# Modulation blocks summed on VectorE ahead of one ones-product, in a decoder trunk with 32 experts

## What is computed

```
mod = SiLU(c) @ w_ada + b_ada          # 6144 columns: shift, scale, gate of two sub-layers
h   = rms(x) * (1 + scale_mix) + shift_mix
z   = h @ w_in                          # [sc_x | sc_B | sc_C | u | v | gate_A | gate_B], 7 x 1024 columns
m   = sigmoid(gate_A) * sc_B * conv3(sc_C * sc_x) + sigmoid(gate_B) * gelu(u) * spatial(LN(gelu(v)))
x   = x + gate_mix * (m @ w_out)
h   = rms(x) * (1 + scale_ffn) + shift_ffn
x   = x + gate_ffn * MoE(h)             # top 4 of 32 experts; then a final norm
```

## Time and profile before

| | |
|---|---|
| median of 3 runs | 1212.75 us (1208.46 to 1213.37) |
| the profiled execution's own time | 1212.76 us |
| its span, first to last instruction | 1211.0 us |
| mean granted TensorE clock | 0.954 |
| TensorE, VectorE, ScalarE busy | 968.6, 452.8, 400.4 us |
| moved by DMA | 467.52 MB, mean 386 GB/s |

### The profile page before, as it was taken

How to read it: one execution, slowest core, us unless ns; L and a number is a source line. 1 busy time by engine, 2 the same in 40 slices (tenths; PEclk the granted TensorE clock), 3 DMA queues, 4 the chain that set the end, 5 groups by cost and what they waited for, 6 DMA issues and landing times.

```text
span 1211.0 us, 23871 instructions
## 1 busy us (share of the span) xinstructions
PE 968.6 (80%) x9321; PEld 495.8 (41%) x9322; DVE 452.8 (37%) x1137; ACT 400.4 (33%) x773; POOL 9.7 (1%) x29
## 2 busy tenths in 40 slices
PE   5999999998688788789689778577587576686586
PEld 3788989853233233234224323123132132132132
DVE  0655654664244244233324324223233233242243
ACT  1544424524243233323324324223223223232234
POOL 0200000000000000000000000000000000000000
PEclk9999999999999899999979989999899899899899
DMA  9979488799989999999997999999999999999993
GB/s 361 376 282 345 171 319 297 293 370 427 425 363 421 426 397 398 425 424 376 425 428 309 426 427 426 426 425 426 428 426 426 426 428 424 425 426 426 425 425 141
DMA packets 60356, 467.52 MB, mean 386 GB/s; under 512 B 5148, under 2 KB 6468, under 8 KB 24484
## 3 DMA queue, kind: packets, MB, share of 16 engines
q1 hardware_dynamic: 60324, 467.06, 93.7%
HBM read 466.00 MB, written 1.05 MB: 386 GB/s over the span
## 4 chain that ended last, share of the span: by engine, by line
PE 48%; DMA 35%; SPq 8%; issue 4%; DVE 4%; ACT 1%; ACTq 0%
DMA W<-in_w_down_dram 33%; PE B L1272 24%; PE B L1019 15%; SPq L385 6%; PE B L1281 3%; PE B L1039 2%; DMA raw<-in_w_in_dram 1%; SPq L387 1%; PE B L1224 1%; DMA raw<-in_w_ada_dram 1%; DVE EW L955 1%; DVE EW L952 1%; DVE EW L958 1%; ACT EW L634 1%; PE B L1287 0%
## 5 line engine op out<-in xcount | busy, mean ns | idle before, releaser
L1272 PE MATMUL B<-W,mT 128*32 128x256 f32 (+1 forms) x5888 | 544.5, 515 | 150.4 <-DMA W<-in_w_gate_up_dram 109.4
L1272 PEld LDWEIGHTS B<-W,mT 128*32 128x32 f32 x5888 | 197.9, 112 | 472.0 <-issue 192.4
L644 ACT ACTIVATE hT<-hT 32x256 bf16<-32x256 bf16 x368 | 152.6, 415 | 241.4 <-DVE hT L972 233.6
L952 DVE TENSOR_SCALAR EW<-B 128x256 f32<-128x256 f32 x46 | 19.5, 425 | 405.3 <-PE B L1272 405.3
L634 ACT ACTIVATE EW<-EW 128x256 f32<-128x256 f32 x46 | 19.2, 416 | 353.7 <-DVE EW L952 353.7
L1019 PE MATMUL B<-hh,wh 128*128 128x256 f32 x384 | 109.9, 286 | 0.0
L1019 PE MATMUL B<-hl,wh 128*128 128x256 f32 x384 | 108.6, 283 | 0.0
L1019 PE MATMUL B<-hh,wl 128*128 128x256 f32 x384 | 108.6, 283 | 0.0
L717 DVE TENSOR_TENSOR wl<-raw,wh 128x2048 fp32r<-128x2048 f32 x32 | 72.7, 2312 | 72.7 <-ACT wh L528 72.7
L1281 PE MATMUL B<-b_gu,mT 128*32 128x512 f32 x368 | 50.2, 614 | 59.9 <-issue 48.4
L528 ACT ACTIVATE wh<-raw 128x2048 fp32r<-128x2048 f32 x32 | 59.6, 1907 | 110.7 <-DMA raw<-in_w_in_dram 76.3
(11 more groups left out here) (241 smaller groups left out, 728.0 us busy)
## 6 DMA issues: line engine op xcount, KB each, us to landing
W<-in_w_gate_up_dram SPq DMA_DIRECT2D x128, 2048.0 KB, 33.6
W<-in_w_down_dram SPq DMA_DIRECT2D x63, 2048.0 KB, 24.8
raw<-in_w_in_dram SPq DMA_DIRECT2D x13, 2048.0 KB, 8.4
raw<-in_w_ada_dram SPq DMA_DIRECT2D x11, 2048.0 KB, 12.1
raw<-in_w_out_dram SPq DMA_DIRECT2D x2, 2048.0 KB, 10.8
W<-in_w_ada_dram SPq DMA_DIRECT2D x1, 2048.0 KB, 24.1
raw<-in_w_in_dram SPq DMA_DIRECT2D x2, 1024.0 KB, 17.0
W<-in_w_down_dram SPq DMA_DIRECT2D x2, 1024.0 KB, 20.4
```

Source lines behind the costliest of these rows:

```text
L644: A(ys[CAP * m:CAP * m + CAP, g * QC:(g + 1) * QC], yp[CAP * g:CAP * g + CAP, m, :], ACT.Copy).then_inc(y_moved, 1)
L952: V.tensor_scalar(halves(gs), paired(GU[:, 0:QC]), LIMIT, None, ALU.min).then_inc(gmin_ready, 1)
L1272: t = M(o, src[:, k % KQ, CAP * (k // KQ):CAP * (k // KQ) + CAP], w, start=(first and k == 0), stop=(k == KT - 1))
```

## The change

The eight units of blocks 1 and 2 are no longer multiplied on TensorE. VectorE weighs them: `weigh(i, q)` multiplies the 128 rows of a contraction step by their 128 values of SiLU(c) (`cT`, one scalar a partition) and adds them into a new tile `weighed` of 128 x 2048. One unit is two instructions; the first of a block writes (TENSOR_SCALAR), all others add (SCALAR_TENSOR_TENSOR). After four units what is left is the sum over 128 partitions, and `sum_weighed(i)` makes it with four matmuls against a tile of ones (`cond[:, 0, :]`, set to 1.0 after block 0 is done). The weighing of a unit stands in VectorE's stream one section ahead of the place that the unit had on TensorE: unit (1, 0) between the splits for SC_C and SC_X; units 1 to 3 of a half behind block 0 of sections 0 to 2; unit (2, 0) behind block 0 of GATE_B of the first half. `ada_used`, which frees the ring slot, now comes from VectorE for these units. Room for `weighed` is made by a smaller scratch for DMA descriptors. The order of the transfers is as before.

```diff
@@ VectorE
+            def weigh(i, q):
+                n = unit_no[("ada", i, q)]
+                dve.wait_ge(*landed(n))
+                if q == 0 and i > 1:
+                    dve.wait_ge(ada_summed, i - 1)
+                w = raw_slot(n).rearrange("p (k j n) -> p k j n", k=2, j=4)
+                if q == 0:
+                    step(V.tensor_scalar(weighed[:, :, :], w[:, 0], cT[:, 0:1], None, ALU.mult))
+                else:
+                    step(V.scalar_tensor_tensor(weighed[:, :, :], w[:, 0], cT[:, 2 * q:2 * q + 1], weighed[:, :, :], ALU.mult, ALU.add))
+                V.scalar_tensor_tensor(weighed[:, :, :], w[:, 1], cT[:, 2 * q + 1:2 * q + 2], weighed[:, :, :], ALU.mult, ALU.add).then_inc(ada_used, 1)
+                dve.wait_ge(ada_used, 4 * i + q + 1)
+                if q == 3:
+                    dve.nop().then_inc(weighed_ready, 1)
...
-                dve.wait_ge(ada_used, 4 * (i + 1))
+                if i == 0:
+                    dve.wait_ge(ada_used, 4)
+                else:
+                    dve.wait_ge(ada_summed, i)
...
             add_bias(0)
+            V.memset(cond[:, 0, :], 1.0).then_inc(ones_ready, 1)
...
-            for j in range(1, 4):
+            for j in range(1, 3):
                 split_low(j)
+            weigh(1, 0)
+            split_low(3)
...
+                        if b == 0 and n < 3:
+                            weigh(1 + h, n + 1)
+                        if b == 0 and s == GATE_B and h + 1 < NH:
+                            weigh(2 + h, 0)
@@ TensorE
+            def sum_weighed(i):
+                if i == 1:
+                    pe.wait_ge(v_gelu, TA * NH)
+                    pe.wait_ge(ones_ready, 1)
+                if i == 2:
+                    pe.wait_ge(mod_ready, 2)
+                pe.wait_ge(weighed_ready, i)
+                for j in range(4):
+                    t = M(B[7][32 * j:32 * j + 32, :], cond[:, 0, :], weighed[:, j, :], start=True, stop=True)
+                t.then_inc(ada_summed, 1)
...
-                        if b == 0 and i < 4:
-                            modulation(1 + h, i)
                     if s == U_:
                         spatial(2 * h + 1)
+                        sum_weighed(1 + h)
@@ build
-    nc = _bacc.Bacc("TRN2", target_bir_lowering=False, num_devices=1)
+    nc = _bacc.Bacc("TRN2", target_bir_lowering=False, num_devices=1, dynamic_dma_scratch_size=2048)
```

More of the change, by code:

```diff
@@ L111, in hybrid_trunk @@
         stat = sb("stat", [P, 64])
+        weighed = sb("weighed", [P, 4, HALF])
         def slot(n, k=1):
@@ L233, in hybrid_trunk @@
         s_slot = [sem(f"s_slot{n}") for n in range(RING)]
-        ada_used = sem("ada_used"); split_h = sem("split_h"); split_l = sem("split_l")
+        ada_used = sem("ada_used"); weighed_ready = sem("weighed_ready"); ada_summed = sem("ada_summed"); ones_ready = sem("ones_ready"); split_h = sem("split_h"); split_l = sem("split_l")
         c_ident = sem("c_ident"); c_iota = sem("c_iota"); c_pcol = sem("c_pcol"); c_late = sem("c_late"); pool_step = sem("pool_step")
@@ L1029, in modulation @@
                     pe.wait_ge(cond_ready, 1)
[L1030 to L1033, removed]
                 n = unit_no[("ada", i, q)]
```

## The result

| | before | after |
|---|---|---|
| median, first comparison | 1210.83 us (4 runs) | 1198.74 us (4 runs) |
| ratio, 95% interval | | 0.990 [0.9873, 0.9927] |
| median, second comparison | 1209.69 us (23 runs) | 1199.06 us (6 runs) |
| ratio, 95% interval | | 0.9906 [0.9886, 0.9926] |
| profiled execution, its own time | 1212.76 us | 1199.81 us |

The change is faster, by 1.0% in the first comparison and 0.9% in the second (0.7 to 1.3% by the intervals).

A forecast was written before the change was run, and what follows sets the result against it. The first stage was taken as bound by TensorE, the experts by transfers. 1212.76 - 14.8 (units removed) + 1.9 (sums added) + 2.4 (TensorE's waits) = 1202.3 us, with a range from 1198.0 to 1209.0 us.

The forecast's parts named there:

- nothing is corrected: Base of the sum: the profiled execution's 1212.76 us was used unadjusted, as the median of the runs was 1212.75.
- The units on TensorE: First stage: eight units of 1.85 us removed, two sums of four matmuls added at 1.9 us together; net 12.9 us less.
- VectorE's operation: One weighing operation over 128x2048 takes w = 2.34 us, a weighing 4.7 us; TENSOR_SCALAR between 1.3 and 2.3 us.
- The layout of the first half: VectorE's splits for SC_B, GATE_A and U_ come 0.3, 1.3 and 2.1 us late; TensorE waits 2.4 us in all.
- The second half: No layer norm there, so VectorE completes U_'s weights with 4 us of room and TensorE does not wait.
- 12d - 4: Extra TensorE wait if a VectorE operation takes d above 2.34 us: 6d in the first half, 6d - 4 in the second.
- Ring and transfers: Weights for GATE_A and U_, waiting for slots freed by weighings, land and are copied with about 3 us to spare.
- The scratch at nothing: The smaller DMA descriptor scratch was put at no effect; if it slowed the ring, the first transfers would show it.
- Everything behind moves along: Behind the first stage, the experts' first issues and all that follows move with TensorE.
- hidden anyway: Rival: the experts' stage is bound by DMA and ends at the same time, 1212.8 us; chance 0.10.
- The clock's rival: TensorE's clock falls after a wait; one section at 1.2 GHz costs 11.7 us more, 1214.0 us; chance 0.02.
- The slower rival: VectorE becomes the bound: gain gone at w = 3.6 us, 1216.9 us at the upper bound of 3.89; chance 0.05.

The follow-up runs named there:

- e4: The change with only block 2, the second half's four units, weighed on VectorE and block 1 left on TensorE: 1203.81 us, ratio to before 0.9962.
- e5: The change with one more TENSOR_TENSOR of 2048 columns on VectorE behind each weighing: 1211.77 us, ratio to before 1.0016.
- e0: The change itself run once more, unaltered, against the kernel before: 1199.06 us, 10.6 us under before.
- e6: The change with weighings 1 to 3 of each half behind the split of their section instead of ahead of it: 1221.88 us, ratio to before 1.0108.
- e1: The kernel before with only the smaller scratch for DMA descriptors: 1209.83 us against 1209.69, ratio 0.9995.
- e3: The change with weighing (1,1) moved from behind the layer norm into its two waits for ScalarE: 1196.79 us, ratio to before 0.9883.

## Why the prediction was right

1202.3 us was forecast with 10.5 us of gain on the profiled execution's 1212.76. Against the 23 runs of before, the change gained 10.6 us. The time itself was 1198.74 and 1199.06 us, over 3 us less than forecast: the base, "nothing is corrected", rested on three runs whose median lay 3.1 us above that of the 23. The direction, the mechanism and the places of the waits were right. Two terms were off by 1 us each, in opposite directions, so that the gain agrees to 0.1 us is luck.

- **The units on TensorE (forecast -14.8 + 1.9 = -12.9 us): mis-sized, it was -13.9.** The one half without waits (e4) shows it clean: 7.1 us at the stage's end, 6.9 with its start 0.2 us earlier. A unit cost 2.03 us, 13.55 for a section with it less 11.52 without; I took 1.85 from the chain and 11.70 as the length of a section's products, and so left the turn back to the products in the section. A sum costs 1.00 us and 0.19 for the same turn back (57.78 against 57.59 us for five sections), and not 0.93. Eight times 2.03 less twice 1.19 is 13.9, and four times 2.03 less 1.19 is e4's 6.9.
- **VectorE's operation (w = 2.34 us): 2.35 us measured**, TENSOR_SCALAR 1.28, at the low end of its 1.3 to 2.3. The step from the rows of 255 and of 2048 elements held. The Trainium skill's rule (page "VectorE: DVE Perf Modes", section "The TRN2 errata"), stated for tensor_tensor, would have given 2.29; for the fused operation the measurement decides, 0.06 us more.
- **The layout of the first half (splits complete at 87.4, 100.1, 113.5): 87.4, 100.2 and 113.8 in the trace.** VectorE's times were right within 0.3 us. The wait was not: 13.9 less the 10.5 gained is 3.4 us, where 2.4 was forecast. The error is again the section's length: with 11.52 us U_'s second half is wanted 0.7 us earlier; 0.3 is VectorE's own. (The waits' row says 3.5 us, but that is another quantity that happens to be near: in that run the v products were done 1.6 us earlier than in the kernel before, and TensorE waited for longer.)
- **The second half (no waits, 4 us of room): no waits.** The room was smaller: with 11.52 us a section it is 3.2, and the split was complete at 183.19 where its second half was wanted at 184.71 + 1.46 = 186.2, so 3.0. The formula 12d - 4 had 1 us too much in its last term, which is 1.0 of the 2.8 us that e5 cost more than expected.
- **Ring and transfers (3 us to spare): less.** GATE_A's w_in was issued at 82.91 us as forecast, but ScalarE's copy shows it landing at 92.1, not 91:

```profile
92.10 3.72 ACT L529 ACTIVATE wh<-raw 128x2048 fp32r<-128x2048 f32 x2 [12.89 <-DMA raw<-in_w_in_dram]
```

  The first copy ends at 94.0 and VectorE came to it at 95.68, so 1.7 us were to spare. At U_ it was closer still. Its w_in was issued at 95.67 as forecast, but only 3.4 us behind another transfer (92.28), and it took 10.8 us and not 8.0:

```profile
106.45 3.72 ACT L529 ACTIVATE wh<-raw 128x2048 fp32r<-128x2048 f32 x2 [10.63 <-DMA raw<-in_w_in_dram]
```

  Landed at 106.45 where 103.6 was forecast, copied at 108.36, and VectorE done with the weighing at 109.13: 0.8 us to spare (0.5 in e0). That the late transfers cost nothing was near to luck. e6 shows what happens when the room is used up.
- **The scratch at nothing:** e1.
- **Everything behind moves along:** the table. The rival "hidden anyway" is out. The clock's rival did not happen in the change: the granted clock from 62 to 116 us, where the waits lie (1.7 us at most), stayed at 1.00:

```profile
62.00:116.00 54.00, 50.45 (x411) 49.33 (x411) 47.14 (x42) 26.67 (x25) 0.00 (x0) 1.00 0.87 317
```

VectorE is busy 47.14 of 54 us there. But its mechanism is real. It came in e5 and e6, and its price in e5, 1.0 us, was far under the 11.7 us of a whole slow section. The slower rival had its mechanism right: e5 with d = 1.16 us stands at the line of no gain, which the sum had put at d = 1.2.

## What to carry to other kernels

When work moves from the bound engine to one with room, lay the receiving engine's stream out instruction by instruction up to each hand-over: here VectorE at 87% busy was enough to make TensorE, the engine that bounds the stage, wait 3.5 us, while 3.4 us a section looked like room. Put the new work into the receiver's own waits (e3: a whole operation in a wait of 2.4 us), and ask of the place both what stands behind it in the stream and what its finish releases: the same operations one step later cost 21 us, through a ring slot. A wait of the bound engine can cost more than its length: in e5 and e6 TensorE's clock fell behind five of six waits from 2.57 to 5.71 us, while it stayed up behind every wait of up to 1.95 us between sections. Read the length of a repeated piece from a stretch without the piece that you remove, or the cost of the turn is counted on the wrong side.

## What the runs showed of the hardware

- Turning TensorE from the 128x256 fp32r products to the 32-column f32 matmuls and back costs 0.13 and 0.18 us, beyond the matmuls' 1.72 us for eight of 512 columns in four strips.
- SCALAR_TENSOR_TENSOR in f32, all operands in SBUF: 484 ns at 255 and 2352 ns at 2048 columns, 1.04 ns an element and 0.22 us fixed; TENSOR_TENSOR has 0.16 us fixed (2289 ns at 2048). TENSOR_SCALAR took 810 ns at 1024 (two scalars a partition) and 1282 ns at 2048 (one), less than half of that for each further element.
- The v products started at 37.6 to 38.2 us in all nine profiles, behind 1.9 to 2.2 us of idle time of TensorE. In three they were done at 59.6 to 59.8 us, in six at 61.0 to 61.6. The difference is the granted clock from 37 to 42 us, 1.00 in the three and 0.66 to 0.74 in the six, and it fell or not in the same kernel, here in the change's first profile and in e0:

```profile
37.00:42.00 5.00, 4.25 (x19) 3.55 (x20) 4.12 (x4) 4.14 (x4) 0.24 (x1) 1.00 1.09 363
```

```profile
37.00:42.00 5.00, 4.22 (x12) 3.34 (x13) 4.20 (x4) 4.21 (x4) 0.28 (x1) 0.66 1.10 364
```

- In the change that did not move the stage's end (235.19 with 59.62, 235.42 with 61.25), since VectorE's stream hung on the transfer that landed at 62.0 and 62.3. TensorE waited 3.5 us in the one and 2.2 in the other by the waits' row. The row says less than the stage lost: without any wait the stage would have ended at 230.2 and 231.8 us, 5.0 and 3.6 us earlier than it did.
